# Last tiles of a stage and first tiles of the next one computed in two groups of 256 tokens at three encoder transitions, with another order and fillers at the last feed-forward

## The chip, the cores and the metric

The kernel runs on one core of a Trainium2 chip. The metric is device time in microseconds (us) of one launch. The engines are named as in the profile: PE (TensorE, matmuls), PEld (its weight loads), DVE (VectorE), ACT (ScalarE), POOL (GpSimd), SP (SyncE, which here only issues DMAs).

## The reference, cut to what matters

512 tokens of width 1024 pass two encoder layers and then a third block with a context of 256 tokens. In each encoder layer:

```
h = rmsnorm(x, norm1_g[l]) * (1.0 + sc1) + sh1
x = x + g1 * token_mix(h, w_in[l], w_fourier[l], w_ret[l], w_out[l])   # its last step: merged @ w_out
h = rmsnorm(x, norm2_g[l]) * (1.0 + sc2) + sh2
x = x + g2 * conv_ffn(h, ffn_up[l], conv_w[l], conv_b[l], ffn_down[l]) # its first step: h @ ffn_up
```

`rmsnorm` sums the squares of all 1024 features of a token, so the norm of any token needs the last tile of the stage before. The third block ends with x + g * rmsnorm(mixer output), a norm of that, and a gated feed-forward (the last feed-forward).

## The kernel before, in words

Activations lie transposed: 8 tiles X[:, t, :] of 128 features by 512 tokens. Each fp32 product is three matmuls (L509 to L511): high part of the weights times high part of the activations, high times low, low times high. So each operand is split: ACT writes the high part (L1528 for weights, L1548 for activations), DVE the low part (L2291, L2333, L2337).

**Weights** come as chunks of 8 blocks of 128x128 (512 KB), in the order in which PE uses them. SP loads chunk i into one of NS = 4 stage buffers (L3459) once DVE has split chunk i - 4. `weights(name, ahead)` on ACT and on DVE splits every chunk up to the one that `name` ends in plus `ahead` (AHEAD = 2), in line with the rest of that engine's program; both queues are in order. The split operands have NW = 3 buffers (WH, WL), except three chunks before the last feed-forward, which go to GH and GL slots 12 to 17 (`early_up`).

**A stage's end.** For each tile n of the stage (token mix: 8 blocks, so 24 matmuls of 512 columns; second half of the feed-forward: 11 blocks, so 33) DVE splits, does a step of the modulation walk (`walk.tick`, L2318: a vector product that belongs to later layers), updates X[:, n] (L2610 or L2658), and adds the square that ACT has made of it to SSQ (L2346). After tile 7 PE issues 4 matmuls that compute nothing (`warm`, L601), the sums over features (L616, L620), 4 more, the spread of the root (L626, after DVE adds EPS in L2362 and POOL takes the power in L3265), and 4 more. Then DVE scales tile by tile (L2379), ACT and DVE split (L1548, L2337), and PE starts the first tiles of the next stage with one block of each per k: `lin2` with two tiles for ffn_up (L550 to L554), `several` with EARLY tiles for w_in (L573 to L577; EARLY[1] = 2).

The three transitions of this kind that the change touches are, by the name of the norm: ("n2", 0), mixer to feed-forward in layer 0; ("n1", 1), feed-forward of layer 0 to mixer of layer 1; ("n2", 1), mixer to feed-forward in layer 1.

**The context load.** SP loads the context (8 DMAs of 128 KB into TAB, L3483) just before chunk `context_at`, and waits for the last matmul of tile ("o", 1, 7) before it:

```
context_at = upto.get(("o", 1, 7), 0) + NS + 1
            if i == context_at:
                sp.wait_ge(mm, "o", 1, 7)
```

**The last feed-forward** already works by halves of 256 tokens (s = 0, 1): the last tile of w_out2 (lines around L1383 to L1396), the residual and its norm (`out_half`, `tile_sum` L1415, x brought through PE by `x_of` and `plus`, L1403 and L1407), and the first three tiles of ffn_w_in (L1480, L1481, L1489). The order on each of PE, ACT, DVE and POOL is written out by hand.

Of the kernel before, what the change touches and what calls it, by code (L numbers as in the profile page):

```python
# [190 lines left out]
def program(nc, ws, wm, xT, cT, params, cond, consts, max_rows, out, plan):  # L191
# [3 lines left out]
    with ctx:  # L195
# [184 lines left out]
        def early_up(i):  # L380

            a = upto.get("early_up")
            return i - a if a is not None and 0 <= i - a < 3 else None
# [8 lines left out]
        def operands_free(i):  # L392

            if early_up(i) is not None:
                return mm, "sum", NH - 1, 5, 1
            i -= NW
            while early_up(i) is not None:
                i -= NW
            return mm, "w", i
# [28 lines left out]
        def split_done(i):  # L428

            if chunks[i][0][0] == "poolm" and chunks[i][0][2] == 0:  # L430
                return whi, "w", i
            return wlo, "w", i

# [51 lines left out]
        def tensor(e):  # L485
# [150 lines left out]

            def token_mix(l):
# [3 lines left out]
                warm(4)  # L641
                rms_first(("n1", l), S, 0, 7)
                warm(4)
                rms_last(("n1", l), S, dv, "aff", ("n1", l), 7)
                warm(4)
# [23 lines left out]
                several([("u", l, g) for g in range(early)], lambda g, k: ("w_in", l, k * 128, g * 128), hx, tiles, ("n1", l))  # L669
# [136 lines left out]
                for n in range(8):  # L806
                    p = take_bank(("o", l, n), dv, "x", "o", l, n)
                    lin(("o", l, n), 8, lambda k: ("w_out", l, k * 128, n * 128), slot, p[:, :], lambda k: ("mg", l, k))

            def conv_ffn(l):  # L810
# [3 lines left out]
                warm(4)  # L814
                rms_first(("n2", l), S, 0, 7)
                warm(4)
                rms_last(("n2", l), S, dv, "aff", ("n2", l), 7)
                warm(4)
# [8 lines left out]
                for half in range(2):  # L827
                    for jj in range(11):
                        j0 = half * 11 + jj
                        if j0 == 0:  # L830
                            pair = [take_bank(("up", l, c), dv, "up", l, c) for c in (0, 22)]
                            lin2([("up", l, 0), ("up", l, 22)],
                                 [lambda k, c=c: ("ffn_up", l, k * 128, c * 128) for c in (0, 22)], hx,
                                 [p[:, :] for p in pair], ("n2", l))
                        else:
                            up(j0)
# [4 lines left out]
                    for n in range(8):  # L841
                        p = take_bank(("dn", l, half, n), dv, "x", "dn", l, half, n)
# [557 lines left out]
            def x_of(t):  # L1400
                p = take_bank(("xs", k1, t), ev, "out+", k1, t, 0)
                pe.wait_ge(dv, "out+", ("ao", 0, 0), t)
                e.matmul(p[:, 0:256], IDN[:, :], X[:, t, 0:256], start=True, stop=False)  # L1403
# [15 lines left out]
            SUM_FIRST, SUM_LAST = [1, 4], [0, 3]  # L1419
# [3 lines left out]
            for s in range(2):  # L1423
                for k in range(8):
# [10 lines left out]
                    if s and k == 1:  # L1435
                        last_sums(0)
                    elif s and k == 5:
                        half_spread(k1, 0)
            walk.tick()
            for nn in range(3, 7):  # L1440
                banks.hand(WOB[nn], ev, "wo", nn)
            for s in range(2):
                banks.hand(LAST_OUT[s], ev, "wo", 7, s)
            x_of(1)
# [9 lines left out]
            tile_sum(5, 0)  # L1454
            tile_sum(2, 0)
            tile_sum(4, 0)
            tile_sum(6, 0)
            tile_sum(3, 0)
            tile_sum(7, 0)
            tile_sum(0, 0)  # L1460
            tile_sum(4, 1)
            tile_sum(0, 1)
            tile_sum(6, 1)
            half_spread(k2, 0)
            tile_sum(1, 1)
            tile_sum(7, 1)
            tile_sum(2, 1)
            close()
            upto["early_up"] = cur["n"] + 1
# [3 lines left out]
            for s in range(2):  # L1473
                for k in range(8):
# [7 lines left out]
                    if s == 0 and k == 0:  # L1482
                        tile_sum(5, 1)
                        tile_sum(3, 1)
                    elif s == 0 and k == 2:
                        half_spread(k2, 1)
                    pe.wait_ge(lo, "h", k2, k, s)
                    for name, (wh, _, chunk, full), p in zip(firsts, parts[k], tiles):
# [3 lines left out]
                        elif s and full:  # L1492
                            done(inst, ("w", chunk))
            close()
# [6 lines left out]
        def scalar(e):  # L1501
# [68 lines left out]

            def token_mix(l):
# [5 lines left out]
                k = ("n1", l)  # L1577
                if l:
                    act.wait_ge(mm, "up", l - 1, 43)
                for t in range(DT):  # L1580
                    affine_one(k, t, S, hx, lambda t: MOD[:, l, t:t + 1])
                    weights((k, t), ahead=0 if l and 3 < t < 6 else 1)
# [20 lines left out]
                def fold_high(g):  # L1603
# [5 lines left out]
                    elif l:  # L1609
                        act.wait_ge(mm, "dn", l - 1, 1, 7)  # L1610
# [129 lines left out]
                for n in range(8):  # L1740
                    weights(("o", l, n))
                    walk.tick()
                    act.wait_ge(dv, "x", "o", l, n)
                    square(("n2", l), n, X[:, n, :], S, first=n == 0)

            def conv_ffn(l):
# [3 lines left out]
                act.wait_ge(mm, "yr", l, 7)  # L1750
                affine(("n2", l), S, hx, lambda t: MOD[:, l, 24 + t:25 + t])
# [3 lines left out]
                for half in range(2):  # L1755
# [22 lines left out]
                    for n in range(8):  # L1778
                        weights(("dn", l, half, n))
                        walk.tick()  # L1780
                        if half:
# [424 lines left out]
            act.wait_ge(mm, "wo", 7)  # L2206
            square_half(1, 0)
            square_half(5, 0)
            square_half(2, 0)
            square_half(4, 0)  # L2210
            square_half(6, 0)
            square_half(3, 0)
            bring(3)
            square_half(7, 0)
            square_half(0, 0)
            square_half(0, 1)
            square_half(4, 1)
# [1482 lines left out]
```

## Time and profile before

| | us |
|---|---|
| median of 3 runs (2971.58 to 2974.42) | 2971.75 |
| the profiled execution's own time | 2975.31 |
| its span | 2973.5 |
| PE busy | 2940.7 (99%) |
| DVE busy | 1787.5 (60%) |
| ACT busy | 1126.8 (38%) |
| POOL busy | 235.7 (8%) |

The profiled time is span plus 1.8 us around it. Starts are in us from the span's start. The lines of a timeline are merged where one instruction follows another of its kind; a matmul's duration is longer than its distance to the next one, since they are pipelined, so the cost of a matmul is read from starts, not from durations.

### The profile page before, as it was taken

The numbers are of one execution on the slowest core, as the hardware profiler recorded it, in microseconds if no ns is written. First come the engines' busy times: TensorE is split into PE (matmuls) and PEld (weight loads), VectorE is DVE, ScalarE is ACT, GpSimd is POOL, SyncE is SP. The second block draws the span as 40 slices with busy tenths as digits, with TensorE's granted clock in tenths as the row PEclk, the third lists the DMA queues.
The fourth block names the chain that finished last, engine by engine and source line by source line (L and its number), as shares of the span: only waits on it lengthen the run. The fifth ranks groups of instructions, "written<-read, shape, count | busy, mean of one in ns | idle before, by whom it ended". The sixth has DMA issues, their size and how long they took to land. (4 is left out here: it accounts for less than half of the span.)

```text
span 2973.5 us, 36519 instructions
## 1 busy us (share of the span) xinstructions
PE 2940.7 (99%) x14873; PEld 2501.1 (84%) x14873; DVE 1787.5 (60%) x2624; ACT 1126.8 (38%) x1704; POOL 235.7 (8%) x198
## 2 busy tenths in 40 slices
PE   7999999999999999999999999999999999999999
PEld 6888888888888888888888889888889887888887
DVE  7767666764867677667856646322347668543233
ACT  4433332433434333323433435222235457432222
POOL 0300000000001200200000011000002006200000
PEclk9999999999999999999999999999999999999999
DMA  7454356344443433344444435222235341222322
GB/s 289 154 184 143 127 181 193 131 139 141 142 135 107 156 126 111 119 140 134 149 138 138 137 118 181 96 100 99 92 113 171 108 149 36 71 80 98 99 94 70
DMA packets 110056, 385.83 MB, mean 130 GB/s; under 512 B 12216, under 2 KB 15672, under 8 KB 109888
## 3 DMA queue, kind: packets, MB, share of 16 engines
q1 hardware_dynamic: 84960, 296.36, 29.8%
q10 hardware_dynamic: 24928, 87.12, 9.0%
q8 instruction: 118, 1.93, 0.3%
q14 instruction: 50, 0.41, 0.0%
HBM read 381.32 MB, written 2.11 MB: 129 GB/s over the span
## 5 line engine op out<-in xcount | busy, mean ns | idle before, releaser
L2291 DVE TENSOR_TENSOR WL<-stage,WH 128x1024 fp32r<-128x1024 f32 x505 | 626.6, 1242 | 557.7 <-ACT WH L1528 557.5
L509 PE MATMUL ps<-HH,WH 128*128 128x512 f32 (+1 forms) x2184 | 851.8, 390 | 0.9 <-DVE WL L2291 0.9
L510 PE MATMUL ps<-HL,WH 128*128 128x512 f32 (+1 forms) x2184 | 848.5, 389 | 0.0
L511 PE MATMUL ps<-HH,WL 128*128 128x512 f32 (+1 forms) x2184 | 848.1, 388 | 0.0
L1528 ACT ACTIVATE WH<-stage 128x1024 fp32r<-128x1024 f32 x509 | 534.6, 1053 | 441.4 <-PE ps L511 428.7
L509 PE MATMUL ps<-GH,WH 128*128 128x512 f32 (+2 forms) x1660 | 572.6, 345 | 3.2 <-DVE WL L2281 2.4
L510 PE MATMUL ps<-GL,WH 128*128 128x512 f32 (+2 forms) x1660 | 571.0, 344 | 0.0
L511 PE MATMUL ps<-GH,WL 128*128 128x512 f32 (+2 forms) x1660 | 571.0, 344 | 0.0
L511 PEld LDWEIGHTS ps<-HH,WL 128*128 128x128 f32 x2184 | 410.0, 188 | 85.6
L509 PEld LDWEIGHTS ps<-HH,WH 128*128 128x128 f32 x2184 | 410.2, 188 | 83.7 <-issue 1.6
L510 PEld LDWEIGHTS ps<-HL,WH 128*128 128x128 f32 x2184 | 410.3, 188 | 81.5
L509 PEld LDWEIGHTS ps<-GH,WH 128*128 128x128 f32 x1660 | 314.2, 189 | 43.0 <-issue 2.9
L510 PEld LDWEIGHTS ps<-GL,WH 128*128 128x128 f32 x1660 | 314.3, 189 | 38.7
L511 PEld LDWEIGHTS ps<-GH,WL 128*128 128x128 f32 x1660 | 314.3, 189 | 37.3
L1548 ACT ACTIVATE GH<-SCR 128x512 fp32r<-128x512 f32 (+5 forms) x310 | 165.9, 548 | 434.2 <-DVE SCR L2528 125.3
L2318 DVE CUSTOM_DVE_ANT_0 MST<-MST,CB,PAR 128x1024 f32<-128x1024 f32 x158 | 204.1, 1292 | 4.5 <-DMA MST<-wm 3.4
L3287 POOL TENSOR_TENSOR GL<-SCR,GH 128x512 fp32r<-128x512 f32 (+3 forms) x102 | 121.2, 1206 | 707.2 <-ACT GH L1548 706.6
L2333 DVE TENSOR_TENSOR GL<-SCR,GH 128x512 fp32r<-128x512 f32 (+1 forms) x192 | 122.1, 644 | 58.9 <-ACT GH L1548 57.2
L3265 POOL TENSOR_TENSOR V<-V,HM 128x4 f32<-128x4 f32 (+1 forms) x23 | 28.7, 1249 | 1395.8 <-DVE V L2362 1395.8
L1767 ACT ACTIVATE SCR<-ps,PAR 128x512 f32<-128x512 f32 x88 | 68.4, 779 | 159.7 <-PE ps L511 158.8
L2775 DVE TENSOR_TENSOR SCR<-ps,SCR 128x512 f32<-128x512 f32 (+1 forms) x66 | 39.7, 601 | 123.3 <-PE ps L511 111.3
L1866 ACT ACTIVATE SCR<-ps 128x512 f32<-128x512 f32 (+1 forms) x66 | 34.8, 527 | 190.8 <-PE ps L511 179.7
(301 smaller groups left out, 2941.6 us busy)
## 6 DMA issues: line engine op xcount, KB each, us to landing
stage<-ws SPq DMA_DIRECT2D x535, 512.0 KB, 3.3
MST<-wm ACTq DMA_DIRECT2D x154, 512.0 KB, 3.3
Z<-wm SPq DMA_DIRECT2D x10, 512.0 KB, 8.0
TAB<-consts ACTq DMA_DIRECT2D x7, 448.0 KB, 3.7
MST<-wm SPq DMA_DIRECT2D x6, 512.0 KB, 7.4
Z<-max_rows ACTq DMA_DIRECT2D x8, 256.0 KB, 4.2
out<-X SPq DMA_DIRECT2D x16, 128.0 KB, 1.8
X<-xT SPq DMA_DIRECT2D x4, 256.0 KB, 5.5
```

Of the source, the lines that this page charges most:

```text
L509: e.matmul(o, wh, mh, start=start, stop=False, **more)
L510: e.matmul(o, wh, ml, start=False, stop=False, **more)
L511: return e.matmul(o, wl, mh, start=False, stop=stop, **more)
L1528: e.activation(wh, src, ACT.Copy).then_inc(whi.sem, whi.up(("w", i)))
L1548: e.activation(dst, src, ACT.Identity if "bias" in more else ACT.Copy, **more).then_inc(hi.sem, hi.up(name))
L1767: e.activation(T, bank("up", l, c)[:, :], ACT.Identity, scale=par("cw", (l * 3 + 1) * 44 + c), bias=par("cb", l * 44 + c)).then_inc(ev.sem ...
L1866: e.activation(T, bank("sa", who, half, jj)[:, 0:n], ACT.Silu).then_inc(ev.sem, ev.up(("sa", who, half, jj)))
L2291: e.tensor_tensor(wl, src, wh.bitcast(F32), ALU.subtract).then_inc(wlo.sem, wlo.up(("w", i)))
L2318: e.tensor_tensor_reduce(out=products, in0=a, in1=b, scale=1.0, scalar=res if i else bias, op0=ALU.mult, op1=ALU.add, accum_out=res).then_inc(
L2333: e.tensor_tensor(dst, src, high_part.bitcast(F32), ALU.subtract).then_inc(lo.sem, lo.up(name))
L2775: made(e.tensor_tensor(T, bank("sb", who, half, jj)[:, 0:n], T, ALU.mult), "sb", who, half, jj)
L3287: e.tensor_tensor(dst, src, high_part.bitcast(F32), ALU.subtract).then_inc(plo.sem, plo.up(name))
```

## The change

Two new functions on PE, each with a partner on ACT, DVE and POOL (`halved`), take the place of the sequence at the three transitions. The last tile of the stage is computed for tokens 0 to 255, then for 256 to 511; the sums and the spread of the first half are issued between the matmuls of the second. Then three first tiles of the next stage (EARLY_UP = (0, 22, 1); EARLY[1] = 3) are computed, 256 tokens at a time. All `warm` calls there are gone. Their three weight chunks use GH and GL slots 12 to 17, so DVE's zeros and ACT's first folded tile in layer 1 wait for ("u", 1, 2). The last tiles' chunks are split further ahead. At the last feed-forward the order of all four engines changes and eight single `warm(1)` are placed.

```diff
+            def last_of_stage(k, name, nk, spec, ready):
+                outs = [take_bank((*name, s), dv, "x", *name, s) for s in range(2)]
+                for s, p in enumerate(outs):
+                    for j in range(nk):
...
+                        inst = mm3(p[:, 0:256], wh, wl, mh[:, half(s)], ml[:, half(s)], j == 0, j == nk - 1)
...
+                        if s and nk == 8:
+                            if j == 1:
+                                first_norm_sums(k, 0)
+                                last_norm_sums(k, 0)
+                            elif j == 5:
+                                norm_spread(k, 0)
+                            elif j == 7:
+                                first_norm_sums(k, 1)
+                        elif s:
+                            if j == 2:
+                                first_norm_sums(k, 0)
+                                last_norm_sums(k, 0)
+                            elif j == 6:
+                                norm_spread(k, 0)
+            def halves(k, names, spec, outs, nk):
+                for s in range(2):
+                    for t in range(8):
...
+                        pe.wait_ge(hi, "h", k, t, s)
+                        for (wh, wl, _, _), p in zip(parts[t], outs):
+                            e.matmul(p[:, half(s)], wh, mh, start=t == 0, stop=False)
+                            e.matmul(p[:, half(s)], wl, mh, start=False, stop=False)
...
+                        pe.wait_ge(lo, "h", k, t, s)
...
@@ scalar and vector, token_mix
                 for n in range(8):
-                    weights(("o", l, n))
+                    if n < 7:
+                        weights(("o", l, n), ahead=AHEAD if n < 5 else n - 2)
...
@@ scalar
+            def halved(k, name, bias, free, nk):
...
+                if nk == 8:
+                    weights(name, ahead=4)
+                    square_half(0)
+                    high_half(0, 0)
+                    high_half(1, 0)
+                    square_half(1)
+                    high_half(2, 0)
+                    weights(name, ahead=5)
+                    high_half(3, 0)
...
@@ vector
+            def halved(k, name, gate, mod, gain, bias, nk):
...
+                scale_of(k, mod, gain)
+                if nk == 8:
+                    weights(name, ahead=4)
+                    x_half(0)
+                    rms_half(0)
+                    affine_half(0, 0)
+                    affine_half(1, 0)
+                    x_half(1)
+                    low_half(0, 0)
...
@@ last feed-forward, PE
-            x_of(1)
-            x_of(3)
-            first_sums(1)
-            last_sums(1)
-            x_of(5)
-            plus(5)
-            plus(1)
-            half_spread(k1, 1)
-            tile_sum(1, 0)
-            plus(3)
...
+            warm(1)
+            tile_sum(2, 0)
+            tile_sum(7, 0)
+            x_of(1)
+            last_sums(1)
+            tile_sum(4, 0)
+            x_of(5)
+            plus(5)
+            half_spread(k1, 1)
+            plus(1)
+            tile_sum(5, 0)
+            x_of(3)
+            tile_sum(0, 0)
+            tile_sum(1, 0)
+            plus(3)
+            tile_sum(6, 0)
+            warm(1)
+            tile_sum(3, 0)
+            warm(1)
+            warm(1)
+            warm(1)
+            warm(1)
+            warm(1)
+            warm(1)
+            half_spread(k2, 0)
+            tile_sum(5, 1)
+            tile_sum(3, 1)
+            tile_sum(1, 1)
```

In `halves`, the sums and the spread of the second half go in among the first three t of s = 0. The split further ahead is the same for ("dn", 0, 1, n). Five of the eight sums of the second half go in among k = 1 and 2 of the first half of the first tiles (two did before, at k = 0), its spread from k = 2 to k = 4. In the last tile of w_out2, `half_spread(k1, 0)` moves from k = 5 to k = 3 and `first_sums(1)` from behind the tile to k = 4.

## Rows read from the trace of the kernel before

**Rows 1.** The page, part 1: busy time of each engine and its share of the span.
```profile
PE 2940.7 (99%) x14873; PEld 2501.1 (84%) x14873; DVE 1787.5 (60%) x2624; ACT 1126.8 (38%) x1704; POOL 235.7 (8%) x198
```
**Rows 2.** Timeline of PE at ("n2", 0): start us, us, engine, line, op [idle before].
```profile
516.50 0.39 PE L509 MATMUL ps<-GH,WH 128*128 128x512 f32 x1
...
521.94 1.03 PE L601 MATMUL ps<-ONR 128*128 128x512 f32 x4
...
528.96 0.48 PE L550 MATMUL ps<-HH,WH 128*128 128x512 f32 x1 [0.93 <-ACT HH L1548]
...
539.98 0.47 PE L509 MATMUL ps<-HH,WH 128*128 128x512 f32 x1
```
**Rows 3.** Timeline of PE at ("n1", 1).
```profile
888.24 1.03 PE L601 MATMUL ps<-ONR 128*128 128x512 f32 x4
...
896.18 0.48 PE L573 MATMUL ps<-HH,WH 128*128 128x512 f32 x1 [0.28 <-ACT HH L1548]
...
907.16 0.46 PE L509 MATMUL ps<-HH,WH 128*128 128x512 f32 x1
```
**Rows 4.** Timeline of PE at ("n2", 1).
```profile
1386.46 1.03 PE L601 MATMUL ps<-ONR 128*128 128x512 f32 x4
...
1405.42 0.47 PE L509 MATMUL ps<-HH,WH 128*128 128x512 f32 x1
```
**Rows 5.** Timeline of PE at the last feed-forward, by halves.
```profile
2574.08 0.28 PE L509 MATMUL ps<-HH,WH 128*128 128x256 f32 x1
...
2576.95 0.50 PE L1383 MATMUL ps<-OC,SSQ 128*128 128x1 f32 x4
2577.32 0.36 PE L509 MATMUL ps<-HH,WH 128*128 128x256 f32 x1
...
2581.22 1.03 PE L1403 MATMUL ps<-X,IDN 128*128 128x256 f32 x4
...
2595.35 0.56 PE L1480 MATMUL ps<-HH,GH 128*128 128x256 f32 x1
...
2603.10 0.28 PE L1480 MATMUL ps<-HH,GH 128*128 128x256 f32 x1
...
2617.13 0.40 PE L509 MATMUL ps<-HH,WH 128*128 128x512 f32 x1
```
**Rows 6.** Timeline of DVE in the last tiles of ("n2", 0).
```profile
516.70 0.75 DVE L2610 SCALAR_TENSOR_TENSOR X<-ps,MOD,X 128x512 f32<-128x512 f32 x1 [0.61 <-PE ps L511]
...
518.15 0.69 DVE L2346 TENSOR_TENSOR SSQ<-SSQ,SCR 128x512 f32<-128x512 f32 x1 [0.70 <-ACT SCR L1561]
519.10 1.23 DVE L2291 TENSOR_TENSOR WL<-stage,WH 128x1024 fp32r<-128x1024 f32 x1 [0.26 <-ACT WH L1528]
520.25 1.28 DVE L2318 CUSTOM_DVE_ANT_0 MST<-MST,CB,PAR 128x1024 f32<-128x1024 f32 x1
```
**Rows 7.** The same in the last tiles of ("n1", 1).
```profile
875.88 0.75 DVE L2658 SCALAR_TENSOR_TENSOR X<-ps,MOD,X 128x512 f32<-128x512 f32 x1
```
**Rows 8.** Timeline of DVE at the last feed-forward: operations on 256 columns.
```profile
2580.78 2.44 DVE L3115 SCALAR_TENSOR_TENSOR SCR<-Z,RC,ps 128x256 f32<-128x256 f32 x6 [1.88 <-PE ps L1396]
```
**Rows 9.** Timeline of ACT at the last feed-forward: a square of 256 columns.
```profile
2577.62 0.42 ACT L2205 ACTIVATE SCR<-Z 128x256 f32<-128x256 f32 x1
```
**Rows 10.** Timeline of SP at ("n2", 1).
```profile
1386.66 3.65 SPq L3483 DMA_DIRECT2D TAB<-cT  x8
1390.35 0.91 SPq L3459 DMA_DIRECT2D stage<-ws  x2
```
**Rows 11.** DMA issues of 1386 to 1394: count, size, median us to landing.
```profile
stage<-ws SPq DMA_DIRECT2D x2, 512.0 KB, 4.9
```
**Rows 12.** The page, part 6: DMA issues of the whole execution, median us to landing.
```profile
stage<-ws SPq DMA_DIRECT2D x535, 512.0 KB, 3.3
```
**Rows 13.** Windows: stretch, its us, busy us of PE PEld DVE ACT POOL, PEclk, DMA share, GB/s.
```profile
892.00:894.00 2.00, 1.70 (x8) 1.70 (x9) 0.00 (x0) 0.00 (x0) 0.24 (x1) 0.54 0.00 0
2590.00:2592.00 2.00, 2.00 (x11) 2.00 (x11) 0.89 (x3) 0.74 (x3) 2.00 (x4) 0.50 0.00 0
```

More of the change, by code:

```diff
@@ L380, in early_up @@
         def early_up(i):
-            a = upto.get("early_up")
-            return i - a if a is not None and 0 <= i - a < 3 else None
+            for k in EARLY_GROUPS:
+                a = upto.get(("early", k))
+                if a is not None and 0 <= i - a < 3:
+                    return i - a
+            return None
+        EARLY_GROUPS = [("n2", 0), ("n1", 1), ("n2", 1), ("an", 2, 0)]
         def operands(i):
@@ L394, in operands_free @@
             if early_up(i) is not None:
-                return mm, "sum", NH - 1, 5, 1
+                g = [k for k in EARLY_GROUPS if ("early", k) in upto and 0 <= i - upto["early", k] < 3][0]
+                if g == ("an", 2, 0):
+                    return mm, "sum", NH - 1, 5, 1
+                if g == ("n1", 1):
+                    return mm, "w", upto["early", ("n2", 0)] + 2
+                return mm, "yr", g[1], 7
             i -= NW
@@ L635, in rms_last, with first_norm_sums @@
                 stat["free"] = (freed_by, freed)
+            def first_norm_sums(k, s):
+                if s:
+                    p = take_bank(("hb", k), dv, "aff", k, 7, 1)
+                else:
+                    stat_free()
+                    p = STAT
+                pe.wait_ge(*added_by(k, 6))
+                for t in (2 * s, 2 * s + 1):
+                    e.matmul(p[:, t:t + 1], SSQ[:, t * 128:t * 128 + 128], OC[:, 0:1], start=t == 2 * s, stop=False,
+                             skip_group_check=True)
@@ L1576, in token_mix @@
                     weights(ahead=AHEAD)
[L1577 to L1582, printed above, removed]
+                    k = ("n1", l)
+                    for t in range(DT):
+                        affine_one(k, t, S, hx, lambda t: MOD[:, l, t:t + 1])
+                        weights((k, t), ahead=1)
                 if l == 0:
@@ L1778, in conv_ffn @@
                     for n in range(8):
-                        weights(("dn", l, half, n))
+                        last = l == 0 and half and n == 7
+                        if not last:
+                            weights(("dn", l, half, n), ahead=AHEAD if l or not half or n < 5 else n - 2)
                         walk.tick()
-                        if half:
+                        if last:
+                            halved(("n1", 1), ("dn", l, 1, 7), lambda t: MOD[:, 1, t:t + 1], ("up", l, 43), 11)
+                        elif half:
                             act.wait_ge(dv, "x", "dn", l, 1, n)
@@ L2232, in scalar @@
             high_half(6, 0)
+            square_half(6, 1)
             high_half(7, 0)
@@ L2397, in token_mix @@
                 k = ("n1", l)
[L2398 to L2407 removed]
+                if l == 0:
                     for t in range(1, 7):
@@ L2654, in conv_ffn @@
                     for n in range(8):
-                        weights(("dn", l, half, n))
+                        if l == 0 and half and n == 7:
+                            walk.need("ada", 1, 0)
+                            walk.need("ada", 1, 1)
+                            dve.wait_ge(modv, "ada", 1, 1)
+                            halved(("n1", 1), ("dn", l, 1, 7), MOD[:, l, 47:48], MOD[:, 1, 8:16], par("n1", 8, 8),
+                                   lambda t: MOD[:, 1, t:t + 1], 11)
+                            walk.tick()
+                            continue
+                        weights(("dn", l, half, n), ahead=AHEAD if l or not half or n < 5 else n - 2)
                         walk.tick()
```

406 lines of the change are left out of this document (304 added, 102 removed).

## Prediction

> **What bounds the kernel now.** I read the page first. PE is busy for 99% of the span [rows 1], so an edit on DVE or ACT is worth only what it lets PE start earlier. PE issues one 512-column matmul per 5.44 / 24 = 0.227 us (516.50 to 521.94 is one tile of 24) [rows 2]. I then read PE's timeline where stages meet. At ("n2", 0) the first useful matmul comes at 528.96, 7.0 us after the last tile ends at 521.94; at ("n1", 1) it comes 7.9 us after (888.24 to 896.18) [rows 2, 3]. PE counts as busy there: `warm` calls, sums and spreads fill the time. The reader is to see that this stretch is a chain of latencies through DVE, ACT, POOL and back, not work. The windows show PE at its higher level (1.00, 2.4 GHz) nearly everywhere; it falls to the lower one (0.50, 1.2 GHz) in thin stretches like 892 to 894 and 2590 to 2592 [rows 13].
>
> **The change, the three transitions, everything hidden.** Counted from the start of the last tile to where two first tiles and a third one are done:
> - ("n2", 0) now: 539.98 - 516.50 = 23.48, and the third tile 5.44: 28.92 us [rows 2].
> - ("n1", 1) now: the tile of 33 matmuls starts 33 x 0.227 = 7.48 before 888.24, at 880.76; 907.16 - 880.76 + 5.44 = 31.84 us [rows 3].
> - ("n2", 1) now: 1405.42 - (1386.46 - 5.44) + 5.44 = 29.84 us [rows 4].
>
> Afterwards a 256-column matmul costs (2576.95 - 2574.08) / 24 = 0.1196 us in a last tile, and (2617.13 - 2603.10) / 117 = 0.1199 in first tiles (13 steps of 9) [rows 5]. So 48 x 0.1196 = 5.74 for 8 blocks, 66 x 0.1196 = 7.89 for 11, and 144 x 0.1199 = 17.27 for three first tiles. The split alone costs 5.74 + 17.27 - 96 x 0.227 = 1.2 us. Sums and spread of a half cost 1.40: 2577.32 - 2576.95 = 0.37 for the first sums, and 2581.22 - 2577.32 = 3.90 for 24 matmuls (2.87) with the last sums and the spread in them, so 1.03 [rows 5]; 2.80 for both. New totals: 25.8, 28.0, 25.8 us. Gains: 3.1, 3.9 and 4.0, in all 11.0 us. DVE's work behind the first tiles, 32 operations at 2.44 / 6, about 0.40 us, is 13 us against 17.3 on PE [rows 8], so it stays hidden once started. `warm` goes and its price (12 x 0.227 = 2.7 us each time) is inside these gains: it lay in a wait.
>
> **What is late next: DVE before the first half's norm.** Tiles 5 and 6 now carry two weight splits each, tile 7 one more before `x_half(0)`. A DVE round is: X at 516.70, SSQ 1.45 later, split at +2.40, walk at +3.55 and 1.29 long, and 0.6 idle until the next X [rows 6]. A second split (520.25 - 519.10 = 1.15) makes the round 5.99 against 5.44, so X of tile 5 is 0.55 late and X of tile 6 1.1 late. `x_half(0)` starts 3.55 after that, at 516.70 + 1.1 + 3.55 = 521.36. It takes some 0.5 until ACT starts and ACT 0.42 [rows 9], so PE can issue the last sums at 522.35. PE is there at 516.50 + 2.87 + 6 x 0.12 + 0.37 = 520.46: a new wait of 1.9 us. PE is in order, so the rest of the tile stands behind it. At ("n1", 1) X of tile 5 starts at 875.88 [rows 7]; with one split more it is 1.15 later, tile 6 follows 1.45 + 0.95 + 2 x 1.15 + 1.29 = 5.99 after, at 883.0, `x_half(0)` at 886.57, the sums at 887.56 against a PE at 880.76 + 3.95 + 9 x 0.12 + 0.37 = 886.16: 1.4 us. At ("n2", 1) it is as in layer 0; every second walk step is two half products there and some 0.4 longer: 2.3 us. Sum 5.6, bounds 0 (splits done early, if DVE's slack of 0.6 a tile took them) and 7.
>
> **What is late next: the load behind the context.** In layer 1, chunk c + 5 (c being tile ("o", 1, 7)'s) is `context_at`: SP first waits for that tile, then issues eight context DMAs (3.65 us from 1386.66), then this chunk (1390.35) [rows 10]. Now nobody needs it for 15 us. In the change ACT's `weights(name, ahead=5)` stands between `high_half(2, 0)` and `high_half(3, 0)` and wants exactly this chunk. With P the end of the last tile on PE, the load is issued at P + 0.2 + 3.65, lands 4.9 later [rows 11], ACT's split takes about as long as DVE's, 1.1 [rows 6], and `high_half(3, 0)` 0.42 [rows 9]: P + 10.2. PE wants it at P + 0.4 + 0.2 + 3 x 1.08 + 1.0 (sums and spread) = P + 4.9. PE waits 5.2 us. Bounds: 3.6 with the usual landing of 3.3 [rows 12], 6 if the thin load is later still. Behind ACT's wait stand all its high parts, so DVE's low parts and PE too. Layer 0 has no such wait on SP.
>
> The profile shows the two loads behind the context landing in 4.9 us against 3.3 elsewhere [rows 11, 12]. The Trainium skill (DMA: Bandwidth & Descriptors, "Queues, rings and completion order") says that each DMA engine takes the descriptors of one issuing queue in ring order, which speaks for the longer one: the chunk's descriptors stand behind 1 MB of context. The same page ("Anatomy of one DMA — SWDGE (gpsimd) path") fits one transfer, on GpSimd's path, at about 2.0 us fixed plus bytes over 436 GB/s, 3.2 us for 512 KB; by that alone the wait would be 3.5 us and not 5.2, and the forecast 1.7 us lower.
>
> **The clock.** No row shows a stall of 5 us at a transition; the thin work from 888.24 on was enough for 0.54 in 892 to 894 [rows 3, 13]. So I count one fall in ("n2", 1): at 1.2 GHz 256 columns take 0.213, 0.094 more than 0.1199. Bounds: 0.9 (the extra width of the bubble in rows 3 against rows 2, which the fall at 892 makes) and 2.5 (27 matmuls, as after 2595.35). I take 1.5.
>
> **The last feed-forward.** Now 2595.35 - 2581.22 = 14.1 us lie between the tile and the first tiles, and those take 21.8 instead of 17.3 [rows 5], for two sums and a spread in them and because the clock is low at first: 2595.35 to 2603.10 are 7.75 us for 27 of those matmuls, two sums and a spread [rows 5]. The new order starts the first half's residual 0.3 us earlier (spread at k = 3 instead of 5), but moves `last_sums(1)` behind two `tile_sum` and one `x_of`, which wait for ACT's squares: the second half's norm comes about 2 us later. Following the new order with these durations at the full clock, `half_spread(k2, 0)` is at 2592.3 and the first tiles run from 2594.1 to 2614.3: 2.8 us gained, if the fillers hold the clock. If it falls shortly before 2590 as now [rows 13], the six fillers take 2.6 instead of 1.4 us, the sums up to twice their time, and the gain is about 0. If it falls already near 2585, since the x tiles are now spread out, the first tiles start at 2600.7: 4.5 us lost. I take 0, the case nearest to the rows; both ends stay in the range.
>
> **The sum.** -11.0 + 5.6 + 5.2 + 1.5 + 0 = +1.3 us. The profiled execution took 2975.31; the median shown is 2971.75, and the difference carries over: 2971.75 + 1.3 = 2973.
>
> **Rivals.**
> 1. *All hidden.* The splits fit DVE's slack, the chunk lands before ACT wants it, and the fillers hold the clock: -11.0 - 2.8 = -13.8, 2958. For it: DVE idles 0.6 us in each round [rows 6]. Against it: a split is 1.15, and SP's order is in the program.
> 2. *Only the load is harmless:* -11.0 + 5.6 = -5.4, 2966.4. For it: ACT reaches its split only in the middle of the first half. Against it: 3.65 us of issuing alone is longer than the three steps.
> 3. *The clock falls early* in the last feed-forward (first at about 2585) and once in one of the other transitions: +1.3 + 4.5 + 1.5 = +7.3, 2979, slower. It decides from the point where PEclk falls before `tile_sum(5, 0)`: every sum, x tile and filler behind it then costs up to twice its time. The new order leaves a pause of some 1.2 us before `tile_sum(2, 0)` and spreads the x tiles. For it: 892 to 894 fell with `warm` on both sides [rows 3, 13]. Against it: the 7.0 us of ("n2", 0) hold no fall [rows 2], with PE waiting as long.
>
> **Chances and range.** Forecast 0.53 (its own range 2969 to 2978), rival 1 0.14, rival 2 0.13, rival 3 0.20. Measurement of this kernel can tell about 0.2%, 5.9 us, from no change: faster means under 2965.8, slower over 2977.7. Faster: all of rival 1, half of rival 2 and a little of the forecast, 0.22. Slower: most of rival 3 and a tail of the forecast, 0.20. Same 0.58. The range 2963 to 2981 leaves out most of rival 1 and the far end of rival 3.
>
> **What would show it.** In PE's timeline afterwards: no L601 at the three transitions; between the two halves of the last tile a pause before the last sums of 1.9, 1.4 and 2.3 us with DVE's split just ahead of `x_half(0)`; 17 us for 144 matmuls in layer 0; in ("n2", 1) a pause of about 5 us at the fourth first-tile step, with ACT waiting for a stage DMA that was issued behind eight context DMAs, and 0.5 in PEclk behind it; in the last feed-forward, first tiles starting between 2594 and 2601 after the shift. I am wrong in the main if that pause is absent (then rivals 1 or 2), or if PEclk stays at 1.00 through the last feed-forward (then 3 us less).

## The result and the profile after

The changed kernel takes 2983.96 us (median of 7 executions, 2978.01 to 2985.57) against 2973.17 us (7 executions beside it): ratio 1.0029, 95% interval 1.002 to 1.0039. It is 0.3% slower; 2973 with a range of 2963 to 2981 was predicted. Its times lie in two groups, 2978.0 and 2978.3, and 2983.2 to 2985.6. The profiled execution is the one of 2978.01, so its trace explains 2.7 us (span 2976.2 against 2973.5) and not the 10.8 of the medians. Run again (e1 below), the profiled execution was one of the long group and its longest, 2987.75 us with a span of 2985.9. Both traces are needed. Three executions further below (one of e7 at 4912.99 us, two of e10 at 3608.88 and 3913.83) had a mean granted clock of 0.56, 0.76 and 0.70 and have no profile; they are left out, which puts the median of e7 at 2965.9 and not 2965.98 and that of e10 at 2974.1 and not 2974.70.

The page, part 1, of the changed kernel (answers to [rows 1]): PE is still 99% busy, so again only PE's own timeline can tell.

```profile
PE 2935.4 (99%) x15142; PEld 2510.7 (84%) x15142; DVE 1795.7 (60%) x2678; ACT 1130.9 (38%) x1731; POOL 240.1 (8%) x201
```

PE's timeline of the changed kernel: start us, us, engine, line, op, [idle before]. L660 and L667 are the first and the last sums of a half, L726 the first tiles. First ("n2", 0), from the start of the last tile to the first full tile after the three first tiles [rows 2]:

```profile
515.93 0.28 PE L523 MATMUL ps<-GH,WH 128*128 128x256 f32 x1
...
519.52 0.50 PE L660 MATMUL ps<-OC,SSQ 128*128 128x1 f32 x4
521.53 0.61 PE L667 MATMUL ps<-OC,SCR 128*128 128x1 f32 x4 [1.50 <-ACT SCR L1711]
...
543.60 0.40 PE L523 MATMUL ps<-HH,WH 128*128 128x512 f32 x1
```

The reader is to see the wait of 1.50 us inside the tile, and 543.60 - 515.93 = 27.67 us where the kernel before had 28.92. ("n1", 1) [rows 3]:

```profile
878.87 0.28 PE L523 MATMUL ps<-GH,WH 128*128 128x256 f32 x1
...
885.52 0.61 PE L667 MATMUL ps<-OC,SCR 128*128 128x1 f32 x4 [1.11 <-ACT SCR L1711]
...
886.91 0.41 PE L525 MATMUL ps<-GH,WL 128*128 128x256 f32 x1
887.12 0.42 PE L523 MATMUL ps<-GH,WH 128*128 128x256 f32 x1
...
909.50 0.40 PE L523 MATMUL ps<-HH,WH 128*128 128x512 f32 x1
```

30.63 us against 31.84. Behind the wait two matmuls of 256 columns start 0.21 us apart (886.91, 887.12), not 0.12: the lower clock. ("n2", 1) [rows 4]:

```profile
1377.84 0.28 PE L523 MATMUL ps<-GH,WH 128*128 128x256 f32 x1
...
1383.77 0.61 PE L667 MATMUL ps<-OC,SCR 128*128 128x1 f32 x4 [1.72 <-ACT SCR L1711]
...
1388.45 0.50 PE L660 MATMUL ps<-OC,SSQ 128*128 128x1 f32 x4
...
1398.38 0.58 PE L726 MATMUL ps<-HH,GH 128*128 128x256 f32 x1 [5.14 <-ACT HH L1682]
...
1413.98 0.40 PE L523 MATMUL ps<-HH,WH 128*128 128x512 f32 x1
```

36.14 us against 29.84. The second wait, 5.14 us, is explained by SP and ACT [rows 10]: eight context DMAs are issued from 1388.65, the chunk behind them at 1393.38, and ACT's split of it starts at 1396.88.

```profile
1388.65 4.69 SPq L3803 DMA_DIRECT2D TAB<-cT  x8
1393.38 1.85 SPq L3779 DMA_DIRECT2D stage<-ws  x4
```
```profile
1396.88 1.06 ACT L1662 ACTIVATE WH<-stage 128x1024 fp32r<-128x1024 f32 x1 [6.41 <-DMA stage<-ws]
```

The last feed-forward [rows 5] takes 41.74 us against 43.05:

```profile
2578.09 0.28 PE L523 MATMUL ps<-HH,WH 128*128 128x256 f32 x1
...
2599.85 0.35 PE L1609 MATMUL ps<-HH,GH 128*128 128x256 f32 x1
...
2619.83 0.40 PE L523 MATMUL ps<-HH,WH 128*128 128x512 f32 x1
```

-1.25 - 1.21 + 6.30 - 1.31 = +2.5 of the 2.7 us.

The windows of the changed kernel, profiled at 2978.01 us (stretch, its us, busy us of PE PEld DVE ACT POOL, PEclk, DMA share, GB/s) [rows 13]: the clock is 1.00 behind the first wait and at or near its lower level (0.50 to 0.58) behind each of the others.

```profile
524.00:528.00 4.00, 3.79 (x34) 3.73 (x33) 3.77 (x11) 2.91 (x6) 0.69 (x1) 1.00 0.02 6
886.00:889.00 3.00, 3.00 (x17) 3.00 (x17) 0.16 (x1) 0.41 (x1) 0.69 (x1) 0.55 0.43 152
1384.00:1388.00 4.00, 4.00 (x23) 4.00 (x23) 0.42 (x2) 0.00 (x0) 0.69 (x1) 0.58 0.00 0
...
1399.00:1401.00 2.00, 2.00 (x11) 2.00 (x11) 2.00 (x6) 1.72 (x5) 0.00 (x0) 0.50 0.65 264
```

The same program in the long group (e1), at ("n2", 0), behind the load wait, and in the last feed-forward:

```profile
522.00:528.00 6.00, 5.98 (x29) 5.99 (x29) 1.08 (x4) 0.76 (x2) 0.70 (x1) 0.51 0.29 91
...
1402.00:1410.00 8.00, 6.64 (x32) 6.64 (x33) 6.66 (x17) 6.27 (x14) 0.00 (x0) 0.53 0.18 74
...
2594.00:2606.00 12.00, 12.00 (x46) 10.92 (x45) 4.13 (x12) 3.72 (x11) 4.75 (x7) 0.50 0.01 1
```

And PE's timeline of it at ("n2", 0): the same wait as above to 0.01 us, and this time the clock falls behind it, 128x256 matmuls 0.21 us apart at 523.23 and 523.44.

```profile
522.02 0.99 PE L667 MATMUL ps<-OC,SCR 128*128 128x1 f32 x4 [1.51 <-ACT SCR L1711]
522.87 0.56 PE L523 MATMUL ps<-GH,WH 128*128 128x256 f32 x1
523.23 0.41 PE L524 MATMUL ps<-GL,WH 128*128 128x256 f32 x1
523.44 0.41 PE L525 MATMUL ps<-GH,WL 128*128 128x256 f32 x1
```

One table of all kernels, us from the start of the last tile to the first full tile after the first tiles, each read from PE's timeline as above (of one profiled execution; the median is of all):

| kernel | median | ("n2", 0) | ("n1", 1) | ("n2", 1) | last feed-forward |
|---|---|---|---|---|---|
| before | 2973.2 to 2973.7 | 28.92 | 31.84 | 29.84 | 43.05 |
| changed | 2983.96 | 27.67 | 30.63 | 36.14 | 41.74 |
| e1 changed, again | 2983.49 | 30.44 | 30.64 | 39.09 | 46.58 |
| e2 transitions only | 2980.81 | 28.93 | 30.64 | 39.23 | 43.03 |
| e3 last feed-forward only | 2974.51 | | | | 46.59 |
| e4 no chunk behind the context | 2973.07 | 27.67 | 30.67 | 29.45 | 43.41 |
| e5 = e4 with late splits | 2966.33 | 26.18 | 28.61 | 26.21 | 40.10 |
| e6 changed, context later | 2974.40 | 28.90 | 30.63 | 29.24 | 41.75 |
| e7 = e5, old last feed-forward | 2965.9 | 26.19 | 28.61 | 26.21 | 43.06 |
| e8 = e3 without fillers | 2979.96 | | | | 44.60 |
| e9 = e4, waits filled | 2970.67 | 27.67 | 29.20 | 28.00 | 46.57 |
| e10 = e5 with the load wait | 2974.1 | 26.19 | 28.59 | 34.12 | 43.43 |
| e11 = e10, wait filled | 2974.21 | 26.18 | 28.60 | 33.41 | 43.42 |
| e12 = e7, old order with fillers | 2967.50 | 26.19 | 28.60 | 26.20 | 44.80 |

### The profile page after: what moved, and what is told of

It is laid out like the page before. It is cut to its first block and busy times, and to the rows that moved or that the text cites. A ratio compares the mean times of both kernels' runs of the same rounds, so it can differ in the third digit from the quotient of the medians.

```text
span 2976.2 us, 37138 instructions
## 1 busy us (share of the span) xinstructions
PE 2935.4 (99%) x15142; PEld 2510.7 (84%) x15142; DVE 1795.7 (60%) x2678; ACT 1130.9 (38%) x1731; POOL 240.1 (8%) x201
## 5 line engine op out<-in xcount | busy, mean ns | idle before, releaser
L2485 DVE TENSOR_TENSOR WL<-stage,WH 128x1024 fp32r<-128x1024 f32 x496 | 617.0, 1245 | 553.0 <-ACT WH L1662 552.7
L523 PE MATMUL ps<-HH,WH 128*128 128x512 f32 x2160 | 842.9, 390 | 1.0 <-DVE WL L2485 0.9
L524 PE MATMUL ps<-HL,WH 128*128 128x512 f32 x2160 | 839.6, 389 | 0.0
L525 PE MATMUL ps<-HH,WL 128*128 128x512 f32 x2160 | 839.1, 388 | 0.0
L1662 ACT ACTIVATE WH<-stage 128x1024 fp32r<-128x1024 f32 x500 | 525.5, 1053 | 452.1 <-PE ps L525 432.8
L523 PE MATMUL ps<-GH,WH 128*128 128x512 f32 (+2 forms) x1687 | 579.4, 343 | 3.6 <-DVE WL L2475 2.4
L523 PEld LDWEIGHTS ps<-GH,WH 128*128 128x128 f32 x1687 | 320.7, 190 | 42.8 <-issue 3.5
L524 PEld LDWEIGHTS ps<-GL,WH 128*128 128x128 f32 x1687 | 320.8, 190 | 37.6
L525 PEld LDWEIGHTS ps<-GH,WL 128*128 128x128 f32 x1687 | 320.8, 190 | 36.2
L2939 DVE SCALAR_TENSOR_TENSOR SCR<-ps,PAR,SCR 128x511 f32<-128x511 f32 x88 | 65.8, 748 | 65.1 <-ACT SCR L1957 65.0
```

Of the source, the lines that this page charges most:

```text
L523: e.matmul(o, wh, mh, start=start, stop=False, **more)
L524: e.matmul(o, wh, ml, start=False, stop=False, **more)
L525: return e.matmul(o, wl, mh, start=False, stop=stop, **more)
L1662: e.activation(wh, src, ACT.Copy).then_inc(whi.sem, whi.up(("w", i)))
L2485: e.tensor_tensor(wl, src, wh.bitcast(F32), ALU.subtract).then_inc(wlo.sem, wlo.up(("w", i)))
L2939: made(e.scalar_tensor_tensor(out=T[:, 1:S], in0=p[:, 0:S - 1], scalar=par("cw", (l * 3) * 44 + c), in1=T[:, 1:S], op0=ALU.mult, op1=ALU.a ...
```

## The experiments

**e1, the changed kernel again.** No edit.

> The changed kernel once more, to catch an execution of its longer kind in a profile. Its seven times lie at two levels, two near 2978.2 and five at 2983.2 to 2985.6, and its profiled execution was of the shorter kind. Theory A (the clock in the last feed-forward): the extra 6 us are a PE clock that falls early in the last feed-forward and stays at half speed for some 12 us more; a profile at the upper level shows 0.50 in PEclk from about 2590 to beyond 2600, and the three transitions as before. Theory B (the wait for the chunk behind the context): the extra 6 us stand right behind that wait, as half speed from 1399 on for some 12 us. If the profile is of the shorter kind again, it tells nothing of the two.

Measured: 2983.49 us (2981.36 to 2987.75), ratio 1.0032 (1.002 to 1.0045). The long group is the usual one, though six more times (2981.36 and up) blur its lower edge. Against the first trace the profiled execution has +2.77 at ("n2", 0), +2.95 at ("n2", 1) and +4.84 in the last feed-forward, 10.6 in all, and -0.9 between the stages: the span's 9.7 us. The first and the last are a clock that is low longer; of the 2.95, 1.75 are a longer wait for the chunk (6.89 against 5.14 us) and 1.2 the clock. So theory A's sign is there and theory B's too, and neither alone: the fall at ("n2", 0) was in neither.

**e2, the change without its edits of the last feed-forward.**

```
-            SUM_FIRST, SUM_LAST = [2, 5], [3, 6]
+            SUM_FIRST, SUM_LAST = [1, 4], [0, 3]
...
```

> The change without its last feed-forward (order of before there, no fillers). From the profile of the changed kernel the three transitions cost -1.2 (27.7 against 28.9), -1.2 (30.6 against 31.8) and +6.3 us (36.1 against 29.8), together +3.9. Theory A: one level, 2973.2 + 3.9 = 2977. Theory B: still two levels, about 2977 and 2983.

Measured: 2980.81 us (2979.96 to 2985.06), 1.0028 (1.0017 to 1.004). Most of the loss is in the transitions. There are two levels as in theory B (four times from 2979.96 to 2981.47, and 2984.84 and 2985.06), some 2 to 3 us higher than expected. The profile is of 2984.84; its wait for the chunk is 7.67 us.

**e3, the edits of the last feed-forward alone.** The reverse of e2's diff.

> The kernel before with only the new order and the fillers at the last feed-forward. In the changed kernel's profile that stretch takes 41.7 us against 43.1. Theory A: two levels, 2973.2 - 1.3 = 2972 in few executions and 2978 in most, so slower than before in the median. Theory B: one level at 2972, a little faster than before.

Measured: 2974.51 us (2970.68 to 2977.44), 1.0004 (0.9995 to 1.0012): no difference in the median, and no level at 2978 for most executions. So theory A falls as the cause of the long group by itself. Its mechanism does occur: the profiled execution, the longest one, has the 46.59 us of e1.

**e4, the changed kernel without the split of the fifth chunk ahead in layer 1** (on ACT and DVE).

```
-                    weights(name, ahead=5)
+                    if k[1] == 0:
+                        weights(name, ahead=5)
...
```

> The changed kernel, in which ACT and DVE do not split the chunk behind the context in the middle of the first tiles of (n2, 1), but after them. Both theories: the wait of 5.1 us at the fourth first-tile step goes, and the transition takes about 31 us instead of 36.1. Theory A: two levels remain, each 5 to 6 us lower, 2973 and 2979. Theory B: one level, 2972 to 2973, since what sets the clock off is gone. If the load was not what ACT waited for, nothing changes.

Measured: 2973.07 us (2971.71 to 2974.42), 0.9998 (0.9989 to 1.0007): 10.4 us back from e1, and one narrow group of times. The wait is gone, ("n2", 1) takes 29.45 us where about 31 were expected. Theory B stands in that the long group goes with this wait. That the wait alone makes it is not shown: in this one profiled execution the clock also happened to hold at ("n2", 0). The narrowness isn't the wait's either: e6 below is without it too and spreads from 2969.88 to 2978.3.

**e5, e4 with the splits ahead of the first half moved behind x_half(0) on DVE and square_half(0) on ACT, no second split in tile 5, and no fifth chunk ahead at the other two transitions either.** A second split stays in tile 6.

```
-                    weights(name, ahead=4)
                     x_half(0)
                     rms_half(0)
+                    weights(name, ahead=3)
...
-                        weights(("o", l, n), ahead=AHEAD if n < 5 else n - 2)
+                        weights(("o", l, n), ahead=AHEAD if n < 6 else 3)
```

> The changed kernel without the fifth chunk ahead (as in e4, 2973.1 us) and with the extra weight splits moved behind x_half(0) on DVE and behind square_half(0) on ACT. Theory P: the waits of 1.5, 1.1 and 1.7 us ahead of the last sums are DVE's second split in tiles 5 and 6 and its split ahead of x_half(0). Then x_half(0) starts as soon as PE's half tile ends, about 0.3 us of each wait is left, (n2, 0) takes about 26.5 us, (n1, 1) 29.8, (n2, 1) 28, and the median is about 2969.5 us. Rival Q: the waits are the latency from PE through DVE and ACT back to PE, not the splits; they stay above 1 us and the median is 2972 or more. A third possibility: the splits, now later, are late for the first tiles; then the waits of the last sums go and new ones stand in the first tiles, with 2973 or more.

Measured: 2966.33 us (2963.41 to 2970.55), ratio 0.9977 (0.9966 to 0.9987): faster than both kernels. Theory P holds, and the time is 3.2 us under its 2969.5: it had left the falls at ("n1", 1) and ("n2", 1) in, 1.5 us each by e9 below, and they went too. Rival Q falls. DVE's timeline of e5: the half x (L2588) follows PE directly, and the split (L2485) comes behind the first half's sums.

```profile
519.20 0.16 DVE L2694 SCALAR_TENSOR_TENSOR AB<-MOD,PAR 128x8 f32<-128x8 f32 x1
519.57 0.48 DVE L2588 SCALAR_TENSOR_TENSOR X<-ps,MOD,X 128x256 f32<-128x256 f32 x1 [0.21 <-PE ps L525]
521.26 0.16 DVE L2595 TENSOR_SCALAR V<-ps 128x2 f32<-128x2 f32 x1 [1.21 <-PE ps L667]
521.55 1.23 DVE L2485 TENSOR_TENSOR GL<-stage,GH 128x1024 fp32r<-128x1024 f32 x1
```

PE's wait ahead of L667 is gone (4 first sums from 520.09, last sums from 520.62), and windows of e5 over the three transitions and the last feed-forward hold no low clock at all:

```profile
518.00:530.00 12.00, 11.77 (x100) 11.63 (x100) 9.32 (x23) 6.26 (x14) 1.39 (x2) 1.00 0.37 130
880.00:892.00 12.00, 11.55 (x98) 11.34 (x97) 7.86 (x19) 5.41 (x12) 2.35 (x2) 1.00 0.37 125
1376.00:1388.00 12.00, 11.75 (x100) 11.61 (x99) 9.43 (x24) 5.91 (x13) 1.39 (x2) 1.00 0.29 84
2566.00:2606.00 40.00, 39.01 (x306) 37.52 (x305) 24.43 (x59) 18.53 (x43) 10.86 (x15) 1.00 0.16 55
```

**e6, the changed kernel with the context loads three chunks later in SP's queue.**

```
-            context_at = upto.get(("o", 1, 7), 0) + NS + 1
+            context_at = upto.get(("o", 1, 7), 0) + NS + 4
```

> The changed kernel with the fifth chunk ahead still there on ACT and DVE, but SP issues the eight context loads three chunks later. Theory: the wait of 5.1 us in (n2, 1) comes from the order of SP's queue alone (it waits for the last tile, then issues the context, then the chunk). Then the chunk is issued before the last tile ends, the wait goes, (n2, 1) takes about 29.5 us as in e4, and the median is about 2973 us. Rival: the chunk waits for its staging buffer, which the splits give back late, or the split itself on ACT is what the first tiles wait for; then a wait of 2 us or more stays and the median is 2976 to 2984 us.

Measured: 2974.40 us (2969.88 to 2978.3), 1.0001 (0.9993 to 1.001). SP's timeline of e6: three chunks are issued before the eight context DMAs.

```profile
1373.29 6.21 SPq L3779 DMA_DIRECT2D stage<-ws  x3
1389.42 4.98 SPq L3803 DMA_DIRECT2D TAB<-cT  x8
```

The split is where it was, and the 5 us wait is gone (29.24 us): it was what stands ahead of the chunk in SP's queue, SP's own wait for the tile and the eight DMAs, which this edit moves together. The three waits of the last sums are the same as before.

**e7, e5 with the last feed-forward of the kernel before.** e5's and e2's diffs together.

> As e5, with the last feed-forward of the kernel before. If the last feed-forward's new order is worth nothing on the median (e3 gave +0.8 us), this is within 1.5 us of e5, about 2969 us. If the new order loses wherever the clock stays low there (46.6 against 43.1 us in e1 and e3), this is 2 us or more below e5, about 2967 us. If the new order gains when the transitions leave the clock alone (43.4 us in e4, 41.7 in the first profile), this is 1 us or more above e5.

Measured: 2965.9 us (2964.4 to 2967.02), 0.9974 (0.9964 to 0.9984). Equal to e5 (0.4 us under it, the intervals overlap): the new order is worth nothing in the median.

**e8, e3 without the eight fillers.**

```
-            warm(1)
             tile_sum(2, 0)
...
-            warm(1)
-            warm(1)
...
             half_spread(k2, 0)
```

> The kernel before with the new order of the last feed-forward, without its eight filler matmuls (e3 with them: 2974.5 us, between 2970.7 and 2977.4). Theory F: the fillers shorten the low clock; without them it is low at least as long as in e3 and the median is 2976 us or more. Rival G: the fillers change nothing in the clock and at 1.2 GHz cost their own time; without them the stretch is about 1 to 2 us shorter, 2973 us. Rival H: neither, within 1 us of 2974.5 us, and the spread of the executions stays as wide.

Measured: 2979.96 us (2974.28 to 2983.22), 1.002 (1.0011 to 1.0028): 5.5 us over e3. The fillers hold the new order up, as theory F says for the median. The mechanism isn't shown: the profiled execution was a short one, with a low clock no longer than in e3 (0.64 and 0.67 in 2584 to 2598, against 0.51 there) and PE waits of 1.32 and 1.04 us that e3 doesn't have.

**e9, e4 with six fillers in the wait ahead of the last sums.**

```
                                 first_norm_sums(k, 0)
+                                warm(6)
                                 last_norm_sums(k, 0)
...
```

> e4 (the changed kernel without the fifth chunk ahead, 2973.1 us) with six filler matmuls of 512 columns on PE ahead of the last sums of the first half, 6 x 0.227 = 1.4 us in each of the waits of 1.5, 1.1 and 1.7 us. The arrival of the square doesn't change. Theory I: the clock falls there because PE stands idle; with the wait filled the falls at 884 and 1384 (1.7 us lost at each in the profile of e4) go, (n1, 1) takes about 29.2 us instead of 30.7, (n2, 1) about 28 instead of 29.5, and the median is about 2970 us. Rival J: the falls come from the thin work around it (sums and spreads of one column) whatever fills the wait, as in the kernel before, which had fillers and fell at 892 and 1388 all the same; then they stay, the fillers cost up to 0.3 us, and the median is 2973 us.

Measured: 2970.67 us (2967.83 to 2973.53), 0.9992 (0.9983 to 1.0), with 29.20 and 28.00 us for the 29.2 and 28 of theory I. The square arrives when it did; PE is only kept busy, and the clock stays up:

```profile
882.00:894.00 12.00, 12.00 (x99) 11.78 (x98) 8.06 (x21) 6.72 (x13) 1.40 (x2) 1.00 0.41 132
1380.00:1392.00 12.00, 11.49 (x91) 10.87 (x90) 8.78 (x23) 5.21 (x12) 1.39 (x2) 1.00 0.36 101
```

So an idle PE of 1.1 to 1.7 us is what lets the clock fall there (e5, without these waits and without fillers, holds it too), and a fall costs 30.67 - 29.20 = 1.47 and 29.45 - 28.00 = 1.45 us on top of the wait. At ("n1", 1) the fillers end 0.14 us after PE could have gone on, so the fall may cost that much more. An idle PE isn't the only thing that a fall follows: the kernel before falls at ("n1", 1) between `warm` calls [rows 3, 13], and at the last feed-forward it, e2, e7 and e12 fall with no wait of PE of 0.2 us or more in the profile.

**e10, e5 with the split of the fifth chunk ahead put back in layer 1.**

```
                     high_half(2, 0)
+                    if k[1]:
+                        weights(name, ahead=5)
                     high_half(3, 0)
...
```

> e5 (2966.3 us, no fall of the clock at a transition) with ACT's and DVE's split of the fifth chunk ahead put back in layer 1, behind the eight context loads on SP. It shows what that wait costs by itself. Theory: the wait of about 5 us and one fall behind it, (n2, 1) at 26.2 + 5.1 + 1.7 = 33 us, median 2972 to 2974 us. Rival: the wait also lets the clock fall later on and costs 10 us as between e1 and e4: 2976 us or more.

Measured: 2974.1 us (2972.76 to 2978.46), 1.0004 (0.9995 to 1.0013): 7.8 us over e5, at the upper end of the theory's 2972 to 2974 and not the rival's 2976. PE's timeline of e10:

```profile
1392.39 0.58 PE L726 MATMUL ps<-HH,GH 128*128 128x256 f32 x1 [5.82 <-ACT HH L1682]
```

34.12 - 26.21 - 5.82 = 2.1 us are the clock behind it. Whether the last feed-forward is longer for it (43.43 against 40.10) or by chance, one profile of each doesn't tell. This wait alone makes no long group: no time is above 2978.46.

**e11, e10 with that wait filled.**

```
+                            if k == ("n2", 1) and t == 3:
+                                warm(20)
                         mh, ml = (x[:, half(s)] for x in hx(t))
```

> e10 with 20 filler matmuls (20 x 0.227 = 4.5 us) on PE in the place where it waits for that chunk. If what the wait costs beyond its own length is the clock that falls behind it, the stretch behind it stays at 2.4 GHz and the median is 1.5 to 3 us under e10. If the cost is the wait alone, both are equal within 0.5 us.

Measured: 2974.21 us (2969.67 to 2976.8), 1.0002 (0.9993 to 1.0011), equal to e10 (2974.1). By the expectation that would mean that the wait alone costs; the traces say something else. The windows of e10 in its wait and behind it:

```profile
1388.00:1392.00 4.00, 0.00 (x0) 0.00 (x0) 0.00 (x0) 1.12 (x2) 0.00 (x0) 0.72 0.92 336
1392.00:1396.00 4.00, 3.61 (x17) 3.61 (x18) 3.63 (x10) 3.47 (x9) 0.00 (x0) 0.50 0.05 22
```

PE's timeline of e11, fillers and wait, and then its windows:

```profile
1387.14 4.53 PE L615 MATMUL ps<-ONR 128*128 128x512 f32 x20
1394.24 0.39 PE L728 MATMUL ps<-HH,GH 128*128 128x256 f32 x1 [2.57 <-ACT HH L1684]
```
```profile
1396.00:1400.00 4.00, 4.00 (x36) 4.00 (x35) 4.00 (x11) 2.54 (x7) 0.00 (x0) 1.00 0.00 0
```

The clock holds (1.00), and ("n2", 1) takes 33.41 - 26.21 = 7.2 us more than in e5, hardly more than the wait; but the wait was 4.53 + 2.57 = 7.1 us here, 1.3 longer than in e10, because the chunk came later: its split on ACT starts 17.8 us after the last tile does, against 16.7. Whether that is chance, one profile doesn't tell, so that the fillers save time here is not shown.

**e12, e7 with eight single fillers between the sums of the residual's tiles.**

```
             plus(3)
+            warm(1)
             tile_sum(5, 0)
+            warm(1)
             tile_sum(2, 0)
...
```

> e7 (late splits, last feed-forward of the kernel before, 2966.0 us) with eight single fillers between the sums of the residual's tiles. Theory F, from e3 and e8 (fillers are worth 5.5 us in the new order): fillers are worth as much in the old order, the clock no longer falls at 2578, the stretch takes 38 to 40 us instead of 43.1 and the median is 2962 to 2964 us, better than e5. Rival K: the old order is paced by ACT and DVE and not by PE's clock, so the fillers lie in the way: 2966 to 2968 us.

Measured: 2967.50 us (2965.2 to 2970.1), 0.9979 (0.9971 to 0.9988), 1.6 us over e7. Theory F doesn't carry over to the old order. K's time holds; its reason, that ACT and DVE set the pace, is not shown, since PE is busy all through. The windows of e7 and of e12 show the clock low as long with the fillers as without, and the stretch is longer by what they take (44.80 against 43.06).

```profile
2578.00:2590.00 12.00, 12.00 (x58) 12.00 (x58) 6.30 (x17) 6.15 (x16) 3.48 (x5) 0.50 0.00 1
```
```profile
2580.00:2594.00 14.00, 14.00 (x69) 13.86 (x69) 6.75 (x19) 6.87 (x17) 3.48 (x5) 0.54 0.00 1
```

## Why the prediction was wrong

The places and the mechanisms of the waits were right: the load wait came within 0.1 us in the first trace, in part by luck (point 3), the waits of the last sums within 0.3 to 0.6. The step that failed is "The clock": "So I count one fall in ("n2", 1)", at 1.5 us. The runs show falls at two transitions in the short execution and at all three in the long one, 4.4 and 8.4 us. Term by term, in us, with what the short execution (first trace) and the usual long one (e1) show:

| term | predicted | short | long |
|---|---|---|---|
| everything hidden | -11.0 | -9.6 | -9.6 |
| waits of the last sums | +5.6 | +3.9 | +3.9 |
| wait for the chunk | +5.2 | +5.1 | +6.9 |
| clock at the transitions | +1.5 | +4.4 | +8.4 |
| last feed-forward | 0 | -1.3 | +3.5 |
| outside these stretches | 0 | +0.2 | -0.7 |
| sum | +1.3 | +2.7 | +12.4 |

1. *Everything hidden*: e5 has neither waits nor a low clock, 26.18, 28.61 and 26.21 us where 25.8, 28.0 and 25.8 were worked out. The gain is 2.74 + 3.23 + 3.63 = 9.6. What is missing at ("n2", 0) and ("n2", 1) includes a wait of 0.21 us for ACT's first high part, at ("n1", 1) one of 0.45 for POOL.
2. *The waits of the last sums*: 1.50, 1.11 and 1.72 us where 1.9, 1.4 and 2.3 were predicted. The durations at full clock say what they cost: 27.67 - 26.18, 29.20 - 28.61 and 28.00 - 26.21 (e9 and e5), 3.9 in all. That the splits are the cause is shown by e5. It moves ACT's as well as DVE's, but DVE's is the late one: in the first trace `x_half(0)` (L2588) starts where DVE's split (L2485) ends, and ACT waits 1.69 us for it. The second split of tile 6, which e5 keeps, does no harm by itself.
```profile
513.53 2.36 DVE L2485 TENSOR_TENSOR GL<-stage,GH 128x1024 fp32r<-128x1024 f32 x2 [0.26 <-ACT GH L1662]
519.40 1.23 DVE L2485 TENSOR_TENSOR WL<-stage,WH 128x1024 fp32r<-128x1024 f32 x1 [0.18 <-ACT WH L1662]
520.54 0.48 DVE L2588 SCALAR_TENSOR_TENSOR X<-ps,MOD,X 128x256 f32<-128x256 f32 x1
521.06 0.42 ACT L1711 ACTIVATE SCR<-X 128x256 f32<-128x256 f32 x1 [1.69 <-DVE X L2588]
```
The size was 0.4 too large at ("n2", 0) because `x_half(0)` starts 4.61 us after the tile (520.54 - 515.93) and not 4.86, and PE is ready 0.14 later.
3. *The chunk behind the context*: 5.14 us in the first trace, for the reason given; e6 shows it. The near match with 5.2 is in part luck: the eight issues took 4.7 us and not 3.65, and from the chunk's issue to ACT's split it was 3.5 and not 4.9. The wait is not a constant: 6.89 us in e1, 5.82 in e10 and 7.1 in e11. From the chunk's issue to the start of ACT's split are 3.5 us in the first trace (1393.38 to 1396.88) and 5.5 in e1 (1396.34 to 1401.86). The fit of the Trainium skill (DMA: Bandwidth & Descriptors, "Anatomy of one DMA — SWDGE (gpsimd) path"), for 512 KB an estimate of 3.2 us, is near the first and far from the second.
4. *The clock at the transitions*: in the first trace 1.43 at ("n1", 1) (30.63 - 29.20), 1.45 ahead of the load wait and 1.55 behind it (36.14 - 28.00 - 5.14 = 3.00 for both). In e1 2.77 at ("n2", 0) (30.44 - 27.67), 1.44, and 39.09 - 28.00 - 6.89 = 4.20. Two things went wrong. The new totals were worked out at the full clock, which took away unseen the falls that the kernel before has at ("n1", 1) [rows 13] and ("n2", 1) and are inside its 31.84 and 29.84 us (the window below is of the kernel before, behind the last tile of ("n2", 1)); in the changed kernel falls at these two places stay, and in e5, where they are gone, the whole gain of 9.6 is there. And the waits of 1.4 to 2.3 us that I had just forecast were priced at their own length, though a PE that waits is what the clock falls behind (e9). The Trainium skill (TensorE: Matmul & The Clock Gate, "Why this matters for your kernels") warns of idle gaps of PE between bursts of matmuls; here pauses of 1.1 and 1.7 us were each followed by a fall in all five profiles that have them, one of 1.5 us in three of five.
```profile
1388.00:1392.00 4.00, 3.64 (x22) 3.18 (x22) 0.16 (x1) 0.08 (x1) 1.01 (x1) 0.81 0.90 236
```

5. *The last feed-forward*: both ends of the range were real. At the full clock 40.2 us were worked out (2574.08 to 2614.3), and e5 shows 40.10; the bad end of 4.5 us lost was nearly reached in e1, e3 and e9 (46.6). Nine profiles of the new order with fillers show 40.10, 41.7 (twice), 43.4 (three times) and 46.6 (three times); three of the old order show 43.0 to 43.1 each. The new order trades a steady 43.05 for a spread around 43.7, which is why e3 and e7 show nothing in the median. The value taken, 0, was about right for it alone (e3 has +0.8 us in the median); with the load wait ahead the long end came up in e1, 3.5 us that the sum had at nothing.

Rival 3 had the sign and the kind of mechanism, with the fall in the last feed-forward "and once in one of the other transitions". It was too small because falls came at all three. The median lies 3 us above the range's 2981, and the clock at the transitions alone is 6.9 us over its term in e1; it is no mechanism that wasn't thought of. What decides whether the clock falls at ("n2", 0) behind the same wait is not settled: it held in the first trace (1.50 us) and in e4 (1.51), and fell in e1 and e2 (1.51 each) and in e6 (1.50). Nor is it shown why the load wait makes the long executions the usual ones: taken out of the changed kernel (e4) it gives back 10.4 us, put into e5 (e10) it costs 7.8.

The way out of it is e5 or e7: 7.2 and 7.6 us under the kernel before, 17 under the changed one.

## What to carry to other kernels

A stage worked out at the full clock silently drops the falls that it has now; keep them in, and price each new wait of PE at its length plus what a fall cost here: 1.5 to 3 us behind waits of 1.1 us and more, though at ("n2", 0) it was nothing in two executions. When a latency chain is to be shortened, let no side task of DVE or ACT stand right ahead of its link (e4 to e5: 6.7 us); one that stands earlier, with slack behind it, may stay, as the second split of tile 6 in e5 does. And look in the queue of the issuing engine for what stands ahead of a load before letting an in-order engine want that load earlier: moving eight DMAs and the wait ahead of them back (e6) was worth 9 us.

## What was not expected of the hardware

- With the same program and the same wait to 0.01 us, the granted clock behind it is 1.00 in one execution and 0.51 for 6 us in another.
- At ("n1", 1) the fall came in every profile that has the wait of 1.1 us (five of five), and in none of the six variants where the wait was filled (e9) or gone (e5, e7, e10 to e12). The kernel before falls there too, between `warm` calls and with no wait over 0.4 us.
- Fillers are worth 5.5 us in one order of the last feed-forward (e8) and cost 1.6 in another (e12): there the clock was low for as long with them.
